# Gathering the rows of two experts at once, with the normed rows as stationary operand

## The chip, the core and the metric

The kernel runs on one core of one Trainium2 chip. The metric is the device time in microseconds of one execution, as a median of several runs. Everything is float32. TensorE (PE) multiplies, VectorE (DVE) and ScalarE (ACT) read the results from PSUM and write them to SBUF, GpSimd (POOL) has small jobs, and SyncE (SP) issues the transfers of the weights. In the tables of the profile a float32 matrix product stands as two MATMUL instructions, each with its own weight load (PEld), and a transpose on PE as one.

## What is computed

One layer of an encoder on 256 tokens of width 1024: two attention branches and their merge, then a mixture of 32 experts of which each token takes 4, then a last norm. The part that matters here is the mixture:

```python
h2 = rmsnorm(x, norm2_g[l])
logits = (xt @ w_router + b_router).astype(jnp.float32)
top_v, top_i = lax.top_k(logits, TOP_K)        # 4 of 32
gates = jax.nn.softmax(top_v, axis=-1)
...
def expert_block(args):                          # rows of the tokens of one expert
    xblk, e = args
    gu = xblk @ w_gu[e] + b_gu[e]                # 1024 -> 2048
    gate = jnp.minimum(gu[:, :D_EXPERT], SWIGLU_LIMIT)
    up = jnp.clip(gu[:, D_EXPERT:], -SWIGLU_LIMIT, SWIGLU_LIMIT)
    act = (up + 1.0) * (gate * jax.nn.sigmoid(SWIGLU_ALPHA * gate))
    return act @ w_down[e] + b_down[e]           # 1024 -> 1024
...
out = jnp.zeros((T + 1, D), jnp.float32).at[row_tok].add(row_w[:, None] * yb.astype(jnp.float32))
```

The weights of one expert are 12 MB: 8 MB for the first product, 4 MB for the second. The 32 experts read 403 MB.

## The kernel before

Each engine runs a program of its own, written out by hand, and semaphores order them. The weights come through a ring of 24 slots of 1 MB in SBUF (`ring`). An expert takes 12 of them: 8 for `up_tile` (one slot is one slice of 128 input channels, gate and up side by side) and 4 for `down_tile`. So the ring holds two experts. SP loads four slots at a time (a group, 4 MB, `group_load`), and a group may be loaded as soon as PE has counted its four slots as read on the semaphore `freed`; the first 24 slots are loaded singly while the attention runs, and the last four singly again. Slot 23 waits for the semaphore `opened`.

The mixture works on blocks of `CAP` = 64 rows for each expert. DVE makes `pick`, a one-hot matrix of tokens by slots, with `build_picks`. In the program `experts(i)` on PE one expert e has, in this order:

- 8 `up_tile`, each with four products (two halves of a bank of PSUM, for `UP` and `GATE`) on the turned rows `xT_e`, and among them the transpose of the routing weights (`turn_gated`) and the biases;
- `scatter`: four products that add the result of expert e-1 to the four banks with the sums of all tokens;
- `gather`: four products with `pick` (128 tokens by 64 slots) as stationary and 512 columns of the normed rows `h2` as moving operand, which put the rows of expert e+1 into the bank `Y`; ACT copies them to `x_e`;
- `turn(act_v)`: four transposes of the activations of e, which DVE then copies to `actT`;
- `turn(x_e, UP)`: four transposes of the rows of e+1, which ACT copies to `xT_e`;
- 8 `down_tile`, two for a slot, which free their slots; ACT copies the result to `y_e`.

The activations of e come from DVE and ACT (`clamp_up`, `clamp_gate`, sigmoid, two products on DVE) while PE scatters and gathers. Ahead of expert 0 stands a prologue: `gather(0, first=True)`, the last of four products that open the sums (`open_sums(1, 1)`, which raises `opened`), `turn(x_e)` and the transpose of all routing weights (`turn_gated(1, Y)`). PE, ACT and DVE loop over the experts two at a time (`UNROLL`), PE with the first and the last two written out.

## Time and profile before

| | before |
|---|---|
| median of 3 runs | 1141.51 us (1140.75 to 1142.64) |
| the profiled execution, its own time | 1142.35 us |
| its span from the first to the last instruction | 1140.4 us |
| mean granted clock of TensorE | 0.998 of full speed |
| PE busy | 1108.2 us, 97% of the span |
| DVE, ACT, POOL busy | 221.8 us, 146.2 us, 30.3 us |
| read from HBM | 433.14 MB, 381 GB/s over the span |

The experts begin at 231.65 us of the span and take nine tenths of what is left of it. PE is busy nearly all of the time, and so are the transfers; which of the two sets the end can't be read from such shares, only from who waits for whom. 1.95 us of the profiled execution's time lie outside its span.

### The profile page before, as it was taken

Reading aid. Unit: us, or ns where it says so; the run is one execution under the profiler, and the core shown is the slowest. Engines: PE = TensorE matmul, PEld = TensorE weight load, DVE = VectorE, ACT = ScalarE, POOL = GpSimd, SP = SyncE. Lnnn points to the kernel's source line nnn. Section 1 sums busy time; section 2 is a strip of 40 time slices with the busy share of each in tenths; the row PEclk is TensorE's granted clock in tenths of the full one; section 3 lists DMA queues with packets and bytes.
Section 4 is the critical chain, followed back from the end, with each engine's and each line's share of the span. In section 5 each row is a group of like instructions: output and inputs, shape, how many; then the busy total and the mean of one; then the engine's idle time right before and its main releaser. Section 6 shows DMA issues by size and latency. Waiting matters only on the chain.

```text
span 1140.4 us, 12368 instructions
## 1 busy us (share of the span) xinstructions
PE 1108.2 (97%) x5162; PEld 451.6 (40%) x5163; DVE 221.8 (19%) x548; ACT 146.2 (13%) x306; POOL 30.3 (3%) x43
## 2 busy tenths in 40 slices
PE   7999999999999999999999999999999999999997
PEld 5858887433333333333333333333333333333332
DVE  1264213321111111111111111111111111111112
ACT  1053120210001100000000000100000000000001
POOL 1250000000000000000000000000000000000000
PEclk9999999999999999999999999999999999999999
DMA  9944366489999999999999999999999999999993
GB/s 361 412 142 179 113 252 223 153 353 409 429 434 428 437 425 438 425 438 426 438 426 438 426 437 428 436 429 434 430 433 431 432 432 431 433 429 434 430 423 132
DMA packets 26725, 434.49 MB, mean 381 GB/s; under 512 B 6416, under 2 KB 6672, under 8 KB 8912
## 3 DMA queue, kind: packets, MB, share of 16 engines
q1 hardware_dynamic: 22208, 430.32, 89.2%
q10 hardware_dynamic: 4496, 3.87, 1.1%
q8 instruction: 15, 0.25, 0.1%
q14 instruction: 6, 0.05, 0.0%
HBM read 433.14 MB, written 1.05 MB: 381 GB/s over the span
## 4 chain that ended last, share of the span: by engine, by line
PE 75%; DMA 22%; ACT 2%; DVE 1%; issue 0%; POOL 0%; DVEq 0%; SPq 0%; POOLq 0%
PE ps L1313 30%; DMA ring<-in_up 21%; PE ps L1327 14%; PE ps L1152 5%; PE ps L1284 4%; PE ps L1335 4%; PE ps L1166 2%; PE ps L1229 2%; PE ps L1041 2%; PE ps L1322 2%; PE ps L1291 1%; ACT work L615 1%; PE ps L1096 1%; PE ps L1060 1%; PE ps L1031 1%; PE ps L1297 1%
## 5 line engine op out<-in xcount | busy, mean ns | idle before, releaser
L1313 PE MATMUL ps<-ring,work 128*64 128x512 f32 x2048 | 461.3, 596 | 12.1 <-DMA ring<-in_up 11.5
L1313 PEld LDWEIGHTS ps<-ring,work 128*64 128x64 f32 x2048 | 141.0, 137 | 301.4 <-issue 281.1
L1327 PE MATMUL ps<-ring,work 128*64 128x512 f32 x1024 | 226.8, 595 | 0.6
L905 DVE TENSOR_SCALAR work<-ps 128x512 f32<-128x512 f32 x32 | 22.1, 692 | 673.6 <-PE ps L1313 673.6
L1327 PEld LDWEIGHTS ps<-ring,work 128*64 128x64 f32 x1024 | 70.7, 137 | 136.1 <-issue 127.9
L1335 PE MATMUL ps<-work 64*128 64x512 f32 x264 | 65.6, 615 | 0.8 <-ACT work L643 0.8
L1284 PE MATMUL ps<-work 128*64 128x512 f32 x264 | 63.9, 605 | 0.1
L1152 PE MATMUL ps<-work,ring 128*128 128x256 f32 x256 | 56.6, 379 | 0.0
L618 ACT ACTIVATE work<-ps 128x256 f32<-128x256 f32 x33 | 12.6, 383 | 336.5 <-PE ps L1297 336.5
L615 ACT ACTIVATE work<-ps 128x512 f32<-128x512 f32 x66 | 39.4, 597 | 104.8 <-PE ps L1284 80.1
L1152 PEld LDWEIGHTS ps<-work,ring 128*128 128x128 f32 x256 | 48.5, 190 | 6.6
L1291 PE MATMUL ps<-const,work 128*128 128x128 f32 x260 | 42.7, 287 | 3.5
L643 ACT ACTIVATE work<-ps 128x512 f32<-128x512 f32 x32 | 19.1, 597 | 208.6 <-PE ps L1327 208.6
L1291 PEld LDWEIGHTS ps<-const,work 128*128 128x128 f32 x260 | 27.4, 141 | 37.6 <-issue 26.0
L637 ACT ACTIVATE work<-work 128x512 f32<-128x512 f32 x32 | 20.2, 630 | 163.4 <-DVE work L902 163.4
L1335 PEld LDWEIGHTS ps<-work 64*128 64x128 f32 x264 | 22.8, 186 | 43.1 <-issue 43.1
L956 DVE COPY work<-ps 128x512 f32<-128x512 f32 x32 | 22.1, 692 | 70.8 <-PE ps L1291 70.8
L1322 PE MATMUL ps<-work 32*64 32x512 f32 x256 | 34.8, 613 | 0.0
L1284 PEld LDWEIGHTS ps<-work 128*64 128x64 f32 x264 | 16.0, 136 | 44.1 <-issue 42.6
L1229 PE MATMUL ps<-ring 128*128 128x512 f32 x64 | 28.5, 595 | 0.0
L1166 PE MATMUL ps<-ring 128*128 128x256 f32 x128 | 28.1, 380 | 0.0
L484 POOL TENSOR_TENSOR sums<-sums,eps 128x1 f32<-128x1 f32 x4 | 2.2, 553 | 966.5 <-DVE sums L834 966.5
(156 smaller groups left out, 540.2 us busy)
## 6 DMA issues: line engine op xcount, KB each, us to landing
ring<-in_up SPq DMA_DIRECT2D x60, 4096.0 KB, 38.1
ring<-in_down SPq DMA_DIRECT2D x29, 4096.0 KB, 35.4
ring<-in_front SPq DMA_DIRECT2D x22, 1024.0 KB, 17.7
ring<-in_up SPq DMA_DIRECT2D x16, 1024.0 KB, 5.4
ring<-in_down SPq DMA_DIRECT2D x12, 1024.0 KB, 9.6
ring<-in_front SPq DMA_DIRECT2D x2, 832.0 KB, 7.9
ring<-in_x SPq DMA_DIRECT2D x2, 512.0 KB, 4.0
ring<-in_x ACTq DMA_DIRECT2D x1, 1024.0 KB, 4.8
```

The costliest lines, as they stand in the source:

```text
L615: return act.activation(dst, ps[:, bank, :], ACT.Copy)
L905: return dve.tensor_scalar(up_c, ps[:, UP, :], LIMIT, -LIMIT, ALU.min, ALU.max)
L1041: last = pe.matmul(ps[:, c // 2, c % 2 * SEQ:(c % 2 + 1) * SEQ], w[:, k % 2, c * P:(c + 1) * P], hT[:, k, :], start=k == 0 and c % 2 == 0, ...
L1152: last = pe.matmul(ps[:, 6 + g % 2, c * SEQ:(c + 1) * SEQ], w[:, k, c * P:(c + 1) * P], hT[:, k, :], start=k == 0, stop=k == KT - 1)
L1166: last = pe.matmul(ps[:, d % 4, m * SEQ:(m + 1) * SEQ], w[:, c, d % 4 * P:(d % 4 + 1) * P], oT[:, 4 * m + c, :], start=c == 0, stop=c == 3)
L1229: return pe.matmul(ps[:, 4 + 2 * t + n, :], gateT[:, k, t * P:(t + 1) * P], w[:, k % 2, n * BANK:(n + 1) * BANK], start=k == 0, stop=k == ...
L1284: last = pe.matmul(ps[n * CAP:(n + 1) * CAP, bank, :], pick[:, b, t, :], h2[:, t, n * BANK:(n + 1) * BANK], start=t == 0, stop=t == TT - 1)
L1291: last = pe.transpose(ps[:, bank, c * P:(c + 1) * P], rows[:, c * P:(c + 1) * P], ident)
L1313: last = pe.matmul(ps[n * CAP:(n + 1) * CAP, bank, :], lhs(xT_e, k), w[bank - GATE][:, n * BANK:(n + 1) * BANK], start=k == 0, stop=k == K ...
L1322: pe.matmul(ps[n * CAP:(n + 1) * CAP, bank, :], expert_row[rows, b, :], up_bias[rows, :], start=False, stop=False, skip_group_check=True)
L1327: last = pe.matmul(ps[n * CAP:(n + 1) * CAP, Y, :], lhs(actT, k), w[:, n * BANK:(n + 1) * BANK], start=k == 0, stop=k == KT - 1, skip_grou ...
L1335: return pe.matmul(ps[:, n, :], gatedT[rows, b, t, :], y_e[rows, :], start=False, stop=False, skip_group_check=True)
```

## The change

The stationary and the moving operand of the gather change places, and two experts are gathered together. A product now has 128 tokens by 128 channels of `h2` as stationary operand and `pick` for two experts (128 tokens by 2 x 64 slots) as moving operand, so the rows arrive in PSUM already turned. Each expert of a pair does half of the pair's eight channel slices for the next pair: one slice ahead of `turn(act_v)` and three behind it. `x_e`, its copy and its transposes are gone; ACT copies one bank for each expert to `xT`, where four half pairs have a place (`homes`). The bank is now `UP`, so that PE waits for DVE's `clamp_up` ahead of it. The last two experts gather nothing. In the prologue all eight slices of the first pair are gathered at once, and the transpose of all routing weights moves behind the second `up_tile` of expert 0. DVE builds the picks of a pair at once, and in the prologue it also copies half of the first pair's rows. The loops of PE, ACT and DVE now take four experts a turn (`UNROLL` is 4, `PAIR` is 2).

```diff
-UNROLL = RING // PER_EXPERT
+PAIR = RING // PER_EXPERT
-TURNS = E // UNROLL
+TURNS = E // PAIR
+UNROLL = 2 * PAIR
...
+        def homes(pair, high):
+
+            if pair % 2:
+                return xT[:, 2:4] if high else xT[:, 0:2]
+            return xT[:, 1:4:2] if high else xT[:, 0:3:2]
...
-            act.wait_ge(gathered, 1)
-            take(x_e).then_inc(xe_ready, 1)
-            act.wait_ge(xT_done, 1)
-            take(xT_e).then_inc(xT_ready, 1)
+            def take_xT(pair, high, bank=UP):
+                return act.activation(homes(pair, high).rearrange("p u k s -> p k u s"),
+                                      ps[:, bank, :].rearrange("p (k u s) -> p k u s", k=4, u=2), ACT.Copy)
+
+
+            act.wait_ge(gathered_low, 1)
+            take_xT(0, 0, MIX).then_inc(xT_ready, 1)
...
-                    act.wait_ge(gathered, e + 2)
-                    take(x_e, Y).then_inc(xe_ready, 1)
-                    act.wait_ge(xT_done, e + 2)
-                    take(xT_e, UP).then_inc(xT_ready, 1)
+                    if not (isinstance(i, int) and e >= E - PAIR):
+                        act.wait_ge(gathered, e + 2)
+                        take_xT(u // PAIR + 1, u % PAIR).then_inc(xT_ready, 1)
...
-            build_picks(0, 0).then_inc(pick_ready, 1)
+            build_picks(0, 0)
+            build_picks(1, 1).then_inc(pick_ready, 1)
             normed(1, 1)
-            build_picks(1, 1).then_inc(pick_ready, 1)
...
+            dve.wait_ge(gathered, 1)
+            dve.tensor_copy(homes(0, 1).rearrange("p u k s -> p k u s"), ps[:, Y, :].rearrange("p (k u s) -> p k u s", k=4, u=2)).then_inc(xT_high, 1)
...
+                    if u % PAIR == 0:
+
+                        dve.wait_ge(gathered, e + 1)
+                        build_picks(0, e + PAIR)
+                        build_picks(1, e + PAIR + 1).then_inc(pick_ready, 1)
...
-                    build_picks(u % 2, e + 2).then_inc(pick_ready, 1)
...
-            def gather(b, bank=MIX, first=False):
+            def picked(bank, q, k, t, first, last):
+
+                return pe.matmul(ps[:, bank, q * 2 * CAP:(q + 1) * 2 * CAP], h2[:, t, k * P:(k + 1) * P], pick[:, t, :], start=first, stop=last,
+                                 skip_group_check=True)
+
+            def gather_first():
+
                 for t in range(TT):
-                    if first:
-                        pe.wait_ge(h2_ready, 2 * t + 2)
-                    for n in range(2):
-                        last = pe.matmul(ps[n * CAP:(n + 1) * CAP, bank, :], pick[:, b, t, :], h2[:, t, n * BANK:(n + 1) * BANK],
-                                         start=t == 0, stop=t == TT - 1)
+                    for k in range(KT):
+                        if k % 4 == 0:
+                            pe.wait_ge(h2_ready, 2 * t + k // 4 + 1)
+                        last = picked((MIX, Y)[k // 4], k % 4, k, t, t == 0 and k % 4 == 0, t == TT - 1)
+                        if t == TT - 1 and k == 3:
+                            last.then_inc(gathered_low, 1)
+                last.then_inc(gathered, 1)
+
+            def gather(k):
+
+                for t in range(TT):
+                    last = picked(UP, k % 4, k, t, t == 0, t == TT - 1)
+                return last
...
-            gather(0, first=True).then_inc(gathered, 1)
+            gather_first()
             open_sums(1, 1).then_inc(opened, 1)
-            pe.wait_ge(xe_ready, 1)
-            turn(x_e).then_inc(xT_done, 1)
-
-            pe.wait_ge(first_gates, 1)
-            turn_gated(1, Y).then_inc(first_ps, 1)
...
-                        up_tile(b, k, use(k), up_done).then_inc(freed, 1)
+                        if static and e == 0 and k == 4:
+                            pe.wait_ge(xT_high, 1)
+                        up_tile(homes(pair, k // 4)[:, b, k % 4, :], k, use(k), up_done).then_inc(freed, 1)
+                        if static and e == 0 and k == 1:
+
+                            pe.wait_ge(first_gates, 1)
+                            turn_gated(1).then_inc(first_ps, 1)
...
+                    following = not (static and e >= E - PAIR)
                     pe.wait_ge(y_ready, e + 1)
                     for n in range(2 * TT):
                         scatter(1 - b, n)
-                    pe.wait_ge(pick_ready, e + 2)
-                    gather(1 - b, Y).then_inc(gathered, 1)
+                    if following:
+                        if b == 0:
+                            pe.wait_ge(pick_ready, i * (UNROLL // PAIR) + (pair + 2))
+                        pe.wait_ge(clamped2, e + 1)
+                        gather(4 * b)
                     pe.wait_ge(gT_ready, e + 1)
                     pe.wait_ge(act_ready, e + 1)
                     turn(act_v).then_inc(actT_done, 1)
-                    pe.wait_ge(xe_ready, e + 2)
-                    turn(x_e, UP).then_inc(xT_done, 1)
+                    if following:
+                        for k in range(4 * b + 1, 4 * b + 4):
+                            last = gather(k)
+                        last.then_inc(gathered, 1)
                     pe.wait_ge(actT_ready, e + 1)
...
-            with pe.Fori(1, TURNS - 1) as i:
+            with pe.Fori(1, E // UNROLL - 1) as i:
                 experts(i)
-            experts(TURNS - 1)
+            experts(E // UNROLL - 1)
```

What this makes of PE's order at two places. First the prologue and the start of expert 0, before (L1284 is `gather`, L1224 `open_sums`, L1291 `turn`, L1297 `turn_gated`, L1313 `up_tile`; here a product is one row):

```order
81 L1224 MATMUL ps<-ring,const 128x512
82 L1284 MATMUL ps<-work 64x512 x4
83 L1224 MATMUL ps<-ring,const 128x512
84 L1291 MATMUL ps<-const,work 128x128 x4
85 L1297 MATMUL ps<-const,work 128x128 x2
86 L1313 MATMUL ps<-ring,work 64x512 x24
87 L1297 MATMUL ps<-const,work 128x128 x2
```

and the same place now (L1299 is the new gather, L1243 `open_sums`, L1335 `turn_gated`, L1351 `up_tile`):

```order
81 L1243 MATMUL ps<-ring,const 128x512
82 L1299 MATMUL ps<-work 128x128 x16
83 L1243 MATMUL ps<-ring,const 128x512
84 L1351 MATMUL ps<-ring,work 64x512 x8
85 L1335 MATMUL ps<-const,work 128x128 x2
86 L1351 MATMUL ps<-ring,work 64x512 x16
87 L1335 MATMUL ps<-const,work 128x128 x2
```

Four wide products and four transposes have become 16 narrow products, and the two transposes of the routing weights now stand behind the second `up_tile`. Second the middle of an expert on PE, before (L1322 the biases, L1335 `scatter`, L1284 `gather`, L1291 both `turn`s, L1327 `down_tile`):

```order
89 L1322 MATMUL ps<-work 64x512 x4
90 L1313 MATMUL ps<-ring,work 64x512 x4
91 L1335 MATMUL ps<-work 128x512 x4
92 L1284 MATMUL ps<-work 64x512 x4
93 L1291 MATMUL ps<-const,work 128x128 x8
94 L1327 MATMUL ps<-ring,work 64x512 x16
```

and now (L1373 `scatter`, L1299 the gather, L1329 `turn(act_v)`, L1365 `down_tile`):

```order
89 L1360 MATMUL ps<-work 64x512 x4
90 L1351 MATMUL ps<-ring,work 64x512 x4
91 L1373 MATMUL ps<-work 128x512 x4
92 L1299 MATMUL ps<-work 128x128 x2
93 L1329 MATMUL ps<-const,work 128x128 x4
94 L1299 MATMUL ps<-work 128x128 x6
95 L1365 MATMUL ps<-ring,work 64x512 x16
```

The four products of 512 columns and the second four transposes are gone, and eight products of 128 columns stand around the first four transposes.

## Rows read from the trace of the kernel before

**Rows 1.** The page, part 4: the chain that ended last, by engine

```profile
PE 75%; DMA 22%; ACT 2%; DVE 1%; issue 0%; POOL 0%; DVEq 0%; SPq 0%; POOLq 0%
```

**Rows 2.** Stretches: length, busy PE, PEld, DVE, ACT, POOL; clock, DMA share, GB/s

```profile
260.00:320.00 60.00, 59.75 (x284) 19.67 (x282) 8.80 (x20) 5.78 (x11) 0.00 (x0) 1.00 1.00 425
...
980.00:1100.00 120.00, 114.47 (x540) 36.99 (x538) 17.60 (x40) 11.22 (x20) 0.00 (x0) 1.00 1.00 432
```

**Rows 3.** Chain that ended last, 960 to 1110 us: start, length, what

```profile
1002.38 49.16 DMA ring<-in_up
...
1060.40 49.43 DMA ring<-in_up
```

**Rows 4.** PE's waits after 255 us: total, times, longest

```profile
PE ps L1313 <- DMA ring<-in_up: 11.5, 10, 1.3
```

**Rows 5.** DMA from 300 to 400 us: instruction queue; transfers, KB, us to landing

```profile
q8 instruction: 2, 0.03, 0.1%
...
ring<-in_up SPq DMA_DIRECT2D x7, 4096.0 KB, 22.0
```

**Rows 6.** The same from 400 to 1050 us, where only one queue is listed

```profile
q1 hardware_dynamic: 9636, 280.66, 100.3%
...
ring<-in_up SPq DMA_DIRECT2D x46, 4096.0 KB, 41.7
```

**Rows 7.** Timeline of SP's issues: start, length, what

```profile
238.92 8.90 SPq L381 DMA_DIRECT2D ring<-in_up  x2
259.72 0.33 SPq L381 DMA_DIRECT2D ring<-in_down  x1
...
287.39 0.33 SPq L381 DMA_DIRECT2D ring<-in_down  x1
```

**Rows 8.** Half microseconds: the stretch, clock, DMA share, GB/s at its end

```profile
260.00:260.50 0.50, 0.50 (x4) 0.14 (x2) 0.00 (x0) 0.17 (x1) 0.00 (x0) 1.00 0.01 0
```

**Rows 9.** Timeline of the prologue and expert 0, PE and DVE

```profile
226.85 0.42 DVE L891 TENSOR_SCALAR work<-const,places 128x64 f32<-128x64 f32 x2
...
227.33 1.94 PE L1284 MATMUL ps<-work 128*64 128x512 f32 x8
...
231.65 10.52 PE L1313 MATMUL ps<-ring,work 128*64 128x512 f32 x48 [0.60 <-ACT work L615]
...
247.22 1.99 PE L1335 MATMUL ps<-work 64*128 64x512 f32 x8
...
252.44 7.09 PE L1327 MATMUL ps<-ring,work 128*64 128x512 f32 x32
```

**Rows 10.** Timeline of PE and PEld at 128x128 stationary operands

```profile
208.06 1.04 PE L1205 MATMUL ps<-const,ring 128*128 128x128 f32 x8
208.93 1.88 PE L1229 MATMUL ps<-ring 128*128 128x512 f32 x4
...
214.65 0.19 PEld L1229 LDWEIGHTS ps<-ring 128*128 128x128 f32 x1 [0.24 <-issue]
...
224.10 0.39 PE L1269 MATMUL ps<-work 128*128 128x32 f32 x2
...
224.32 0.39 PE L1270 MATMUL ps<-work 128*128 128x32 f32 x2
```

**Rows 11.** Timeline of the last expert on DVE: the activations

```profile
1120.15 0.69 DVE L954 TENSOR_TENSOR work<-work 128x512 f32<-128x512 f32 x1
```

**Rows 12.** Chain that ended last, in the last expert

```profile
1113.53 0.37 PE ps L1297 x2
...
1118.65 1.92 PE ps L1335 x8
1120.57 1.89 PE ps L1284 x8
...
1122.48 0.61 ACT work L615
...
1123.13 0.66 PE ps L1291 x4
```

More of the change, by code:

```diff
@@ L162, in build @@
         soft = sb("soft", [P, 2, 8])
-        routing = sb("routing", [P, TT, E + UNROLL])
+        routing = sb("routing", [P, TT, E + PAIR])
         places = sb("places", [P, TT, ROUNDS * E])
@@ L217, in build @@
         h2 = held(0, TT, D)
-        x_e = held(2048, BANK)
-        xT_e = held(2560, BANK)
-        gate_c, up_c, sig, y_e = (held(3072 + n * BANK, BANK) for n in range(4))
+        xT = held(3072, 4, 4, CAP)
+        xT_over = held(3072, KT, CAP)
+        gate_c, up_c = (held(2048 + n * BANK, BANK) for n in range(2))
+        sig, y_e = (held(4096 + n * BANK, BANK) for n in range(2))
         actT, act_v = gate_c, up_c
-        pick = held(5120, 2, TT, CAP)
+        pick = held(5120, TT, 2 * CAP)
         gated = held(5376, 2, TT, P)
@@ L233, in build @@
         part_rows = held(3744, TT, P)
[L234 to L236 removed]
+        logits, struck = (held(4096 + n * TT * (E + TOP), TT, E + TOP) for n in range(2))
+        best, strike = (held(4240 + n * TT * 8, TT, 8) for n in range(2))
+        chosen, expo = (held(4272 + n * TT * E, TT, E) for n in range(2))
         gf = flat[:, PER_EXPERT * SLOT:PER_EXPERT * SLOT + D]
@@ L317, in through, with fine @@
             return FIRST[name] + dict(FRONT)[name]
+        def homes(pair, high):
+            if pair % 2:
+                return xT[:, 2:4] if high else xT[:, 0:2]
+            return xT[:, 1:4:2] if high else xT[:, 0:3:2]
+        def fine(turn, at):
+            return turn == 0 or turn == TURNS - 1 and at >= RING - SPAN
         block = ctx.enter_context(nc.Block())
@@ L381, in group_load, with fine_load @@
                 sp.dma_start(ring[:, SPAN * g:SPAN * (g + 1), :], unit(i, g)).then_inc(grouped[g], 16)
+            def fine_load(i, at):
+                sp.wait_ge(freed, i * RING + (N_FRONT - RING + at + 1))
+                expert_load(i, at)
             with sp.Fori(1, TURNS - 1) as i:
@@ L659, in _ @@
                             act.wait_ge(v_gathered, k + 1)
-                            take(x_e).then_inc(v_xe, 1)
-                            act.wait_ge(v_xTd, k + 1)
-                            take(xT_e).then_inc(v_xT, 1)
+                            act.activation(xT_over, ps[:, MIX, :].rearrange("p (k s) -> p k s", k=KT), ACT.Copy).then_inc(v_xT, 1)
                             act.wait_ge(v_gTd, k + 1)
@@ L890, in build_picks @@
                 for t in range(TT):
-                    last = dve.tensor_scalar(pick[:, b, t, :], slots, places[:, t, bass.ds(je, 1)], None, ALU.is_equal)
+                    last = dve.tensor_scalar(pick[:, t, b * CAP:(b + 1) * CAP], slots, places[:, t, bass.ds(je, 1)], None, ALU.is_equal)
                 return last
@@ L1355, in experts @@
                     b = u % 2
+                    pair = u // PAIR
                     def use(j):
-                        at = u * PER_EXPERT + j
-                        if isinstance(i, int) and (i == 0 or at >= RING - SPAN):
-                            pe.wait_ge(loaded[at], 16 * (front_loads(at) + 1 + (i > 0)))
+                        at = u % PAIR * PER_EXPERT + j
+                        turn = i * (UNROLL // PAIR) + pair
+                        if static and fine(turn, at):
+                            pe.wait_ge(loaded[at], 16 * (front_loads(at) + sum(fine(n, at) for n in range(turn + 1))))
                         elif at % SPAN == 0:
-                            pe.wait_ge(grouped[at // SPAN], i * 16)
+                            pe.wait_ge(grouped[at // SPAN], i * (16 * UNROLL // PAIR) + 16 * (pair))
                         return halves(at)
                     for k in range(KT):
-                        up_tile(b, k, use(k), up_done).then_inc(freed, 1)
+                        if static and e == 0 and k == 4:
[4 more added lines that the diff above has]
+                            turn_gated(1).then_inc(first_ps, 1)
                         if k == 5:
                             pe.wait_ge(gated_ready, e + 1)
+                            if static and e == 0:
+                                pe.wait_ge(y_ready, 1)
                             turn_gated(b).then_inc(gT_done, 1)
@@ L1409, in _ @@
                             pe.wait_ge(v_pick, k + 1)
-                            gather(0).then_inc(v_gathered, 1)
-                            pe.wait_ge(v_xe, k + 1)
-                            turn(x_e).then_inc(v_xTd, 1)
+                            gather_over().then_inc(v_gathered, 1)
                             pe.wait_ge(v_xT, k + 1)
@@ L1416, in _ @@
                             for j in range(KT):
-                                last = up_tile(0, j, halves(j), v_up)
+                                last = up_tile(xT_over[:, j, :], j, halves(j), v_up)
                                 if j == 0:
```

38 lines of the change are left out of this document (19 added, 19 removed).

## Prediction

> **What bounds the kernel now.** I read the chain that ended last first. It gives PE three quarters of the span and the transfers 22% [rows 1], and a busy PE beside a busy DMA says no more. So I went along the chain in order of time. In its last third it has a piece of transfer of some 49 us in each turn of two experts, which ends at 1051.54 and again at 1109.83 us [rows 3]: 58.29 us for two experts, 29.15 us for one. SP's issues show the other rate: a down group is issued when PE has freed its slots, at 259.72 and at 287.39 us [rows 7], so early on PE needs 27.67 us for an expert. PE is the faster one, by 1.48 us an expert. It doesn't wait at first because the ring starts full, and it eats this lead up.
>
> Three more views say that the transfers are the limit all along. The DMA share is 1.00 from 260 us on, with 425 to 432 GB/s, whether PE waits or not [rows 2]. The time from issue to landing of an up group grows from 22.0 us (300 to 400 us) to 41.7 us (400 to 1050 us) [rows 5, 6], where 4 MB alone take 4.19 MB / 432 GB/s = 9.7 us: orders pile up in the queue. And PE's waits for the weights come to 11.5 us in all [rows 4]; that is the whole sum by which PE would be ahead. The time then is: when the transfers become continuous, plus a fixed 90 groups less two, plus what PE does after the last up group has landed.
>
> The Trainium skill, page "DMA: Bandwidth & Descriptors", section "Where 436 GB/s comes from", puts the ceiling of the ports at 435 GB/s. By that the 432 GB/s can't get better, and no faster PE draws more from them.
>
> **The price of a narrow product.** The new instruction is a load of 128x128 float32 and 128 moving columns; a product is two of them. Before has none exactly so. Eight transposes, each with a load of 128x128 and 128 moving columns, take 208.93 - 208.06 = 0.87 us until the next product starts, 0.109 us each [rows 10]. Products with the same stationary operand and only 32 columns, two instructions, follow each other at 0.22 us (224.10, 224.32), 0.11 each [rows 10]. The load of 0.19 us hides behind 0.43 us of 512 columns (0.19 busy, 0.24 idle) [rows 10]. I take 0.112 us. From below it can't be under 0.107, since 512 columns take 0.43. From above, load and pass one after the other would be 0.19 + 0.107 = 0.297 us; loads that follow each other but hide the pass, 0.19. The short pairs lie at the low end.
>
> **An expert on PE.** Before, from the start of `scatter` to the start of `down_tile`: 252.44 - 247.22 = 5.22 us [rows 9]. In it lie gather 1.89, the wait for ACT's copy 0.61 and the turn of `x_e` 0.66 [rows 12]. Now: scatter 1.92, first slice 4 x 0.112 = 0.45, turn of the activations 4 x 0.109 = 0.43, three slices 12 x 0.112 = 1.34; in all 4.14 us, a gain of 1.08 an expert. Do new waits appear? The activations are ready at 1120.15 + 0.69 = 1120.84, 2.2 us after the scatter's start at 1118.65 [rows 11, 12]; PE is there after 2.37. DVE's copy to `actT` (a pass over 512 columns like that of 0.69 us [rows 11]) hides behind the three slices (1.34); without them it would be the wait it is in the tail below. `clamp_up` is over before the scatter ends. ACT's copy has the 7.09 us of `down_tile`, and DVE's four picks stand where DVE waits for PE. So 27.67 becomes 26.59 us, against 29.15 for the transfers. These 31 x 1.08 = 33.5 us go into PE's wait for weights, which becomes 11.5 + 33.5 = 45 us, and not into the time.
>
> **The prologue.** DVE makes two picks (0.42 us) before PE starts at 227.33, and the second pair of picks comes ahead of it now [rows 9]: PE starts at 227.75. 32 instructions x 0.112 = 3.58, `open_sums` two passes at 0.43 = 0.86: expert 0 starts at 232.19 instead of 231.65 [rows 9]. ACT's copy of the low half (behind 24 instructions, at 230.44, plus 0.6) is done by then; DVE's half, at 231.3 plus 0.7, is wanted 7 us later. The routing sums that DVE now does behind this copy are wanted behind the second `up_tile`, 3.6 us after the start. The transposes of the routing weights add 0.37 [rows 12] ahead of the third slot. The first group is freed 0.54 + 0.37 = 0.91 us later, and SP issues it at 239.8 instead of 238.92 [rows 7]. `opened` comes 2 us later too; slot 23 is wanted only at the end of expert 1, and behind it the DMA had been idle before 238.92 anyway.
>
> The second group is queued behind the first, so both end 0.91 later. The third, issued at 259.72 [rows 7], changes by 0.91 - 1.08 = -0.2. Before, nothing moved from 260.0 to 260.5 [rows 8], between the end of the second and the start of the third; with the third already queued this gap of about 0.6 us goes. The transfers become continuous 0.91 - 0.6 = 0.3 us later (between -0.6, if the start of the pipe shortens too, and 0.9).
>
> **The tail.** The last up group lands at 1109.83 [rows 3]. The last expert gathers nothing: from 1120.57 PE would go to the turn of the activations at about 1120.9, and then takes 0.66 + 0.69 + 0.08 = 1.43 for turn, copy and start. `down_tile` starts at 1122.3 instead of 1123.79 (1123.13 + 0.66 [rows 12]): 1.5 us less. Its weights, 9.7 us behind the last up group, are there at 1119.5.
>
> **Sum.** + 0.3 - 1.5 = - 1.2 us. On the profiled execution: span 1140.4 to 1139.2, with the 1.95 us outside it 1142.35 to 1141.2. The median of the runs stands 0.8 us below that execution: 1141.5 - 1.2 = 1140.3 us. A difference of 0.2% (2.3 us) is about what can be told from no change; this is under it.
>
> **The rivals.**
>
> *PE is the bound, and gets its gain.* The chain's 75% speak for it: -33.5 - 1.2 gives 1106.8 us. Against it stand the landing times and the DMA share. 3 in 100.
>
> *The transfers gain too.* At 260 to 320 us they had 425 GB/s and later 432 [rows 2]. If a queue that fills sooner cures that, it is 60 x 7 / 432 = 1.0 us; with the gap gone and no delay at the front (-0.6), the sum is -0.6 - 1.0 - 1.5 = -3.1: 1138.4 us. For it speaks only that the slow stretch is the one with few orders waiting. 12 in 100.
>
> *Slower: the stationary load isn't hidden.* At price x an expert costs 16 (x - 0.112) more. PE has 45 us to give away over 31 experts, 496 instructions: up to x = 0.112 + 45/496 = 0.203 only the prologue's 32 instructions count (at 0.19 us +2.5, which gives 1142.8, no measurable change). Beyond it PE is the bound. At 0.297: 496 x 0.185 - 45 = +46.8, prologue +5.9, rest -1.2, so 1193 us. It decides at 0.203. Against it is 0.109 of the transposes. 6 in 100.
>
> The Trainium skill speaks for this rival: page "TensorE: Matmul & The Clock Gate", section "The mechanism", says that a weight load overlaps running products only when its row group differs (or, a sentence earlier, in the background buffer). Here all use all rows, so by the stricter sentence it would be 0.297 and 1193 us. The 0.43 spacing with 0.19 of load in it contradicts that sentence.
>
> *Slower: the transfers lose rate.* PE now reads four times as many stationary columns for the gather while the weights stream in. If they stayed at the 425 GB/s of the first stretch [rows 2] for the 850 us of the stream, it is 850 x 7 / 432 = +14 us, 1154 us. In these rows the rate doesn't follow what PE does. 3 in 100.
>
> *Slower: the longer loop is fetched again at each turn.* Before, 400 to 1050 us list no instruction queue at all [rows 6], while 300 to 400 still has two packets [rows 5]; the body stays, with 130 MATMULs and as many loads an expert and two experts, some 520 instructions. Now it is 134 and 134 for each of four, about 1070. With five jumps back and 45 us to give away, a jump must cost over 9 us to be seen; at 10 us each the time is 1140.3 + 5 = 1145. 2 in 100.
>
> The Trainium skill, page "Runtime: NRT & Kernel Launch", section "Instruction fetch mechanics", says that a jump out of a window of two pages of 256 instructions stalls. The body before is already beyond two pages, and no fetch is seen.
>
> **How the numbers follow.** My case has 74 in 100; its own range is 1139.2 (both bounds low, -0.6 - 1.5 and x = 0.107) to 1142.8 (x = 0.19). The faster cases, with 1138.4, are taken in below; above, the scatter of the runs themselves, 1140.75 to 1142.64, is added to 0.6 of delay. Range 1138.2 to 1143.4. Faster by over 0.2% means under 1139.2: 3 + 12 = 15. Slower, over 1143.8: 6 + 3 + 2 = 11. Within: 74.
>
> **What would show it.** Right: an expert's PE work from scatter to `down_tile` at 4.1 us; 32 instructions of the prologue in 3.6 us; PE's waits for weights near 45 us and beginning before 600 us; the last up group landing within 1 us of 1109.8 at 432 GB/s; from there to the end 29.1 instead of 30.6 us. Wrong: a spacing near 0.3 us in the gather, an expert's period over 29.15 us with no DMA wait, instruction packets between 400 and 1050 us with idle PE, or a DMA share under 1.00 after 260 us.

## The result and the profile after

The changed kernel is a little slower: 1143.59 us against 1141.64 us (medians of 17 runs each), a ratio of 1.0018 with a 95% interval of 1.0010 to 1.0025, that is +2.0 us (1.1 to 2.9). Forecast was -1.2 us, with a range of 1138.2 to 1143.4 us. The profiled execution after took 1143.02 us, its span is 1141.2 us; for the one of before that is 1142.35 and 1140.4 us.

The chain that ended last, by engine, and the stretches of the profile after (columns as in [rows 2]):

```profile
PE 59%; DMA 38%; DVE 1%; ACT 1%; issue 0%; POOL 0%; DVEq 0%; SPq 0%; POOLq 0%
```

```profile
260.00:320.00 60.00, 60.00 (x302) 22.16 (x300) 8.88 (x20) 5.01 (x9) 0.00 (x0) 1.00 1.00 428
...
500.00:620.00 120.00, 120.00 (x598) 44.31 (x596) 17.76 (x40) 9.81 (x18) 0.00 (x0) 1.00 1.00 433
620.00:740.00 120.00, 114.49 (x562) 41.35 (x560) 19.01 (x42) 8.83 (x16) 0.00 (x0) 0.99 1.00 431
...
980.00:1100.00 120.00, 110.61 (x528) 38.96 (x525) 17.77 (x40) 8.23 (x15) 0.00 (x0) 0.97 1.00 431
```

The transfers run as before, at 431 to 433 GB/s [rows 2]. New is the clock: from 620 us on its mean is under 1.00. PE's waits, the transfers' landing between 400 and 1050 us, and SP's issues (a queue of the kind "instruction" carries code to an engine; I call its entries code packets, and the profile doesn't say for which engine they are):

```profile
PE ps L1351 <- DMA ring<-in_up: 25.0, 17, 2.8
```

```profile
q8 instruction: 3, 0.05, 0.0%
q14 instruction: 1, 0.01, 0.0%
...
ring<-in_up SPq DMA_DIRECT2D x47, 4096.0 KB, 48.7
```

```profile
240.45 8.89 SPq L393 DMA_DIRECT2D ring<-in_up  x2
260.35 0.33 SPq L393 DMA_DIRECT2D ring<-in_down  x1
...
287.13 0.33 SPq L393 DMA_DIRECT2D ring<-in_down  x1
```

The orders pile up higher (48.7 instead of 41.7 us, [rows 6]), an expert takes PE 26.78 us (260.35 to 287.13) instead of 27.67 [rows 7], and PE waits 25.0 us instead of 11.5 [rows 4], the first time at 643 us and not before 600. PE's timeline of the prologue, of expert 0 and of its end:

```profile
228.02 3.84 PE L1299 MATMUL ps<-work 128*128 128x128 f32 x32 [0.46 <-DVE work L903]
231.69 1.02 PE L1243 MATMUL ps<-ring,const 128*128 128x512 f32 x2
232.65 3.65 PE L1351 MATMUL ps<-ring,work 128*64 128x512 f32 x16
236.23 0.44 PE L1335 MATMUL ps<-const,work 128*128 128x128 f32 x2
...
248.74 1.99 PE L1373 MATMUL ps<-work 64*128 64x512 f32 x8
250.66 0.71 PE L1299 MATMUL ps<-work 128*128 128x128 f32 x4
251.20 0.60 PE L1329 MATMUL ps<-const,work 128*128 128x128 f32 x4
251.64 1.50 PE L1299 MATMUL ps<-work 128*128 128x128 f32 x12
253.07 7.09 PE L1365 MATMUL ps<-ring,work 128*64 128x512 f32 x32
```

From `scatter` to `down_tile` it is 253.07 - 248.74 = 4.33 us (5.22 before), and the loads of 128x128 are hidden: 32 instructions in 3.67 us, 0.115 each.

**Where an execution differs by chance.** Two profiles of one kernel differ already in the attention part, and this moves everything behind it. The first products start at 6.94 to 7.24 us, by when x has landed; more comes from the 32 instructions behind the first transposes, which take 12.42 us in the first profile of the changed kernel and 11.39 us in its second. Why isn't shown. So the stages are counted from a mark: the start of the first products of the output projection (L1229, now L1248). The table takes them from the profile of each run; "first group" is SP's first group of four slots, "last up" the landing of the last up group, "down" the start of the last eight down tiles. "Last wait" is PE's wait ahead of the last up group. The kernels below the fourth row are those of the experiments.

| kernel | mark | first group - mark | last up - mark | last wait | last up to down | down to end |
|---|---|---|---|---|---|---|
| before | 190.89 | 48.03 | 918.94 | 1.26 | 13.97 | 16.6 |
| before, again | 191.07 | 48.03 | 918.95 | 1.24 | 13.97 | 16.6 |
| after | 191.26 | 49.19 | 919.55 | 1.03 | 12.66 | 17.7 |
| after, again | 190.25 | 49.19 | 919.72 | 2.75 | 14.36 | 17.8 |
| fill_end | 190.08 | 49.19 | 919.77 | 0.21 | 12.67 | 16.6 |
| pad_real | 190.90 | 49.19 | 919.54 | 2.64 | 12.67 | 16.6 |
| before_tail | 189.93 | 48.02 | 919.06 | 1.25 | 12.57 | 16.5 |
| fine_turn1 | 190.03 | | 916.62 | 3.06 | 14.08 | 17.5 |
| best | 190.31 | | 916.52 | 0.22 | 12.66 | 16.5 |
| prologue_twice | 190.20 | 52.76 | 923.10 | 2.65 | 14.36 | 16.5 |
| pad_pe | 191.11 | 49.19 | 919.50 | 0.99 | 12.67 | 17.7 |
| pad_act | 189.82 | 49.19 | 919.50 | 2.65 | 14.31 | 18.0 |
| fill_end2 | 189.82 | 49.19 | 919.52 | 0.20 | 12.67 | 16.6 |
| pad_early | 190.65 | 49.19 | 921.91 | 0.99 | 12.67 | 16.6 |

Three columns tell of the change: the last group lands 0.6 to 0.8 us later, the way to the last down tiles is 1.3 us shorter or 0.4 us longer, and what follows is 1.1 to 1.2 us longer.

### The profile page after: what moved, and what is told of

Read it like the earlier page. It is cut to its first block, busy times and chain, and to the rows that moved or that the text cites. A ratio compares the mean times of both kernels' runs of the same rounds, so it can differ in the third digit from the quotient of the medians.

```text
span 1141.2 us, 12513 instructions
## 1 busy us (share of the span) xinstructions
PE 1095.8 (96%) x5278; PEld 482.9 (42%) x5279; DVE 223.8 (20%) x549; ACT 125.4 (11%) x271; POOL 30.3 (3%) x43
## 4 chain that ended last, share of the span: by engine, by line
PE 59%; DMA 38%; DVE 1%; ACT 1%; issue 0%; POOL 0%; DVEq 0%; SPq 0%; POOLq 0%
DMA ring<-in_up 38%; PE ps L1351 24%; PE ps L1365 9%; PE ps L1171 5%; PE ps L1299 3%; PE ps L1185 2%; PE ps L1248 2%; PE ps L1060 2%; PE ps L1373 2%; PE ps L1360 2%; PE ps L1115 1%; PE ps L1079 1%; PE ps L1050 1%; PE ps L1335 1%; PE ps L1088 1%; PE ps L1329 1%
## 5 line engine op out<-in xcount | busy, mean ns | idle before, releaser
L1351 PE MATMUL ps<-ring,work 128*64 128x512 f32 x2048 | 474.8, 609 | 25.0 <-DMA ring<-in_up 25.0
L1351 PEld LDWEIGHTS ps<-ring,work 128*64 128x64 f32 x2048 | 142.2, 139 | 326.1 <-issue 285.9
L1365 PE MATMUL ps<-ring,work 128*64 128x512 f32 x1024 | 226.8, 595 | 1.6 <-DVE work L976 1.6
L1365 PEld LDWEIGHTS ps<-ring,work 128*64 128x64 f32 x1024 | 70.6, 137 | 133.7 <-issue 128.0
L1299 PEld LDWEIGHTS ps<-work 128*128 128x128 f32 x512 | 61.8, 191 | 24.0 <-issue 22.7
L1299 PE MATMUL ps<-work 128*128 128x128 f32 x512 | 70.3, 281 | 0.5 <-DVE work L903 0.5
L1373 PE MATMUL ps<-work 64*128 64x512 f32 x264 | 65.6, 615 | 0.7 <-ACT work L657 0.7
L1171 PE MATMUL ps<-work,ring 128*128 128x256 f32 x256 | 56.6, 379 | 0.0
L1171 PEld LDWEIGHTS ps<-work,ring 128*128 128x128 f32 x256 | 48.5, 190 | 6.6
L657 ACT ACTIVATE work<-ps 128x512 f32<-128x512 f32 x32 | 19.1, 597 | 212.0 <-PE ps L1365 212.0
L1373 PEld LDWEIGHTS ps<-work 64*128 64x128 f32 x264 | 22.7, 186 | 43.1 <-issue 41.5
L634 ACT ACTIVATE work<-ps 128x512 f32<-128x512 f32 x31 | 18.5, 597 | 93.6 <-PE ps L1299 93.6
L1248 PE MATMUL ps<-ring 128*128 128x512 f32 x64 | 28.5, 595 | 0.0
L1060 PE MATMUL ps<-work,ring 128*128 128x256 f32 x128 | 27.8, 379 | 0.0
L1060 PEld LDWEIGHTS ps<-work,ring 128*128 128x128 f32 x128 | 24.3, 190 | 3.6 <-issue 0.3
```

The source lines that it names most:

```text
L1060: last = pe.matmul(ps[:, c // 2, c % 2 * SEQ:(c % 2 + 1) * SEQ], w[:, k % 2, c * P:(c + 1) * P], hT[:, k, :], start=k == 0 and c % 2 == 0, ...
L1171: last = pe.matmul(ps[:, 6 + g % 2, c * SEQ:(c + 1) * SEQ], w[:, k, c * P:(c + 1) * P], hT[:, k, :], start=k == 0, stop=k == KT - 1)
L1248: return pe.matmul(ps[:, 4 + 2 * t + n, :], gateT[:, k, t * P:(t + 1) * P], w[:, k % 2, n * BANK:(n + 1) * BANK], start=k == 0, stop=k == ...
L1299: return pe.matmul(ps[:, bank, q * 2 * CAP:(q + 1) * 2 * CAP], h2[:, t, k * P:(k + 1) * P], pick[:, t, :], start=first, stop=last, skip_gr ...
L1351: last = pe.matmul(ps[n * CAP:(n + 1) * CAP, bank, :], x, w[bank - GATE][:, n * BANK:(n + 1) * BANK], start=k == 0, stop=k == KT - 1, skip ...
L1365: last = pe.matmul(ps[n * CAP:(n + 1) * CAP, Y, :], lhs(actT, k), w[:, n * BANK:(n + 1) * BANK], start=k == 0, stop=k == KT - 1, skip_grou ...
```

## The experiments

**The two kernels again.**

> The kernel before, once more, to see which differences of two single profiles are the draw of one execution. Three such differences lie between the profile of before and that of after: the attention part starts 0.36 us later in after, already at the first matrix product behind the load of x; the output stores have a hole of 1 us; the last up group lands 0.97 us later. Every theory: ratio 1.000 within 0.1%. If the first two are draws, they differ between the two profiles of before as well, by 0.3 us and about 1 us.

Measured: 1141.75 us, ratio 0.9999 (0.9990 to 1.0008). Its stages are those of before to 0.02 us; only the mark moved. So the slow end of the stores, which I had thought a draw of one execution, is none.

> The changed kernel, once more. Theory A (clock): PE now waits longer for each up group, and behind such waits its granted clock falls to half for some 3 us, as at 1081.67 us of the first profile, where 16 up products took 5.32 instead of 3.65 us. In the stream that costs nothing, but behind the very last wait it lengthens the tail by 1.67 us. Then this profile should show the fall behind the last up group in some executions, and the ratio is 1.0018 again. Theory B (prologue): the delay at the first group, 1.2 us net of the draw, is all there is; then the span from the last up group to the end is 29.2 us plus the draw of the stores, and the ratio can't be over 1.000.

Measured: 1144.08 us, ratio 1.0021 (1.0012 to 1.0030). Theory A's fall of the clock is there behind the last up group. PE's up tiles behind a wait, in the two profiles of the changed kernel (first the first one, with the turns before; then the second):

```profile
818.04 5.35 PE L1351 MATMUL ps<-ring,work 128*64 128x512 f32 x16 [2.15 <-DMA ring<-in_up]
847.18 3.65 PE L1351 MATMUL ps<-ring,work 128*64 128x512 f32 x16 [0.44 <-DMA ring<-in_up]
876.33 5.35 PE L1351 MATMUL ps<-ring,work 128*64 128x512 f32 x16 [2.16 <-DMA ring<-in_up]
...
1052.54 3.65 PE L1351 MATMUL ps<-ring,work 128*64 128x512 f32 x16 [2.79 <-DMA ring<-in_up]
1081.67 5.32 PE L1351 MATMUL ps<-ring,work 128*64 128x512 f32 x16 [2.13 <-DMA ring<-in_up]
1110.85 3.65 PE L1351 MATMUL ps<-ring,work 128*64 128x512 f32 x16 [1.03 <-DMA ring<-in_up]
```

```profile
1080.75 3.65 PE L1351 MATMUL ps<-ring,work 128*64 128x512 f32 x16 [2.15 <-DMA ring<-in_up]
1110.01 5.35 PE L1351 MATMUL ps<-ring,work 128*64 128x512 f32 x16 [2.75 <-DMA ring<-in_up]
```

and the stretches of 1 us of the second (clock third from the end):

```profile
1109.00:1110.00 1.00, 0.00 (x0) 0.00 (x0) 0.00 (x0) 0.00 (x0) 0.00 (x0) 1.00 0.95 393
1110.00:1111.00 1.00, 0.99 (x4) 0.44 (x6) 0.00 (x0) 0.00 (x0) 0.00 (x0) 0.66 0.96 401
1111.00:1112.00 1.00, 1.00 (x4) 0.24 (x2) 0.00 (x0) 0.00 (x0) 0.00 (x0) 0.50 1.04 434
1112.00:1113.00 1.00, 1.00 (x4) 0.24 (x2) 0.00 (x0) 0.00 (x0) 0.00 (x0) 0.50 1.02 426
```

The 16 instructions take 3.65 us, or 5.35 us with the clock at 0.50 (1.2 GHz instead of 2.4), and never the longer time behind a wait of 0.44 us. Behind a wait of over 2 us the clock mostly falls, not always: behind 14 of the 19 such waits of these two profiles. In the stream it costs nothing: the 1.7 us come out of the next wait, which is then 0.4 us. Behind the last wait they are paid. In the first profile the clock fell one wait earlier, at 1081.67 us, so that the last wait was only 1.03 us long and no fall followed; in the second it fell behind the last wait itself. The same holds for the other profiles in which no wait was filled: behind a last wait of 2.65 to 3.06 us it fell (fine_turn1, pad_act, prologue_twice), behind one of 0.99 us it didn't (pad_pe, pad_early). Only pad_real, with a last wait of 2.64 us and no fall, stands out.

**The gather in the experts twice.**

```diff
             def gather(k):

-                for t in range(TT):
-                    last = picked(UP, k % 4, k, t, t == 0, t == TT - 1)
+                for _ in range(2):
+                    for t in range(TT):
+                        last = picked(UP, k % 4, k, t, t == 0, t == TT - 1)
```

> The changed kernel with each narrow product of the gather inside the experts issued twice (the second overwrites the first with the same numbers; the prologue gathers once): 16 x 0.112 = 1.8 us more PE work for an expert, 28.6 us against 29.15 for its transfers, so PE's waits nearly vanish. Theory A (clock behind waits): faster than the changed kernel by 1 to 2 us, ratio to before 0.999 to 1.000, and a mean clock of 0.998. Theory B (prologue): the same as the changed kernel, ratio 1.0018, since the prologue and the tail are unchanged. If PE were the bound it would be 30 x 1.8 = 54 us slower.

Measured: 1153.85 us, ratio 1.0109 (1.0094 to 1.0125), and no wait of PE for weights at all.

```profile
307.36 1.16 PE L1299 MATMUL ps<-work 128*128 128x128 f32 x8
308.36 0.60 PE L1330 MATMUL ps<-const,work 128*128 128x128 f32 x4
308.79 2.84 PE L1299 MATMUL ps<-work 128*128 128x128 f32 x24
311.57 7.09 PE L1366 MATMUL ps<-ring,work 128*64 128x512 f32 x32
```

Both expectations were wrong, because I compared one expert with one transfer and forgot the lead that the full ring gives the transfers at the start. 16 instructions more cost 1.79 us an expert (28.57 instead of 26.78), for 30 experts 53.7 us. The median is 9.8 to 10.3 us over the changed kernel's, but this run has neither of the two extra costs at the end that are found below (16.6 us from down to end, mean clock 0.999). By the stages, the last down tiles start 944.5 us after the mark instead of 932.2 (after) and 932.4 (fill_end), 12.1 to 12.3 us later. So PE had 41.4 to 41.6 us to give away, where the prediction has 45. What the clock costs it can't tell.

**Single loads in the second turn.**

```diff
         def fine(turn, at):

-            return turn == 0 or turn == TURNS - 1 and at >= RING - SPAN
+            return turn <= 1 or turn == TURNS - 1 and at >= RING - SPAN
...
-            with sp.Fori(1, TURNS - 1) as i:
+            for at in range(RING):
+                fine_load(1, at)
+            with sp.Fori(2, TURNS - 1) as i:
...
-                            pe.wait_ge(grouped[at // SPAN], i * (16 * UNROLL // PAIR) + 16 * (pair))
+                            pe.wait_ge(grouped[at // SPAN], i * (16 * UNROLL // PAIR) + 16 * (pair) - 16)
```

> The changed kernel with the 24 slots of the second turn loaded singly, each as soon as PE has freed it, instead of four at a time. Both theories have the transfers as the bound from 260 us on: they now go on as soon as slot 0 is free (234.5 us) and slot 23 has landed (about 237 us), instead of at 240.45 us, so the last up group lands 3 to 4 us earlier, if the single loads keep 432 GB/s, and the time falls by as much: ratio to before 0.998 to 0.999. If the gap of the DMA between 236.8 and 240.5 us were hidden anyway, nothing changes.

Measured: 1140.74 us, ratio 0.9996 (0.9987 to 1.0005), 3.3 us under the changed kernel beside it. The last up group lands 3.0 us earlier after the mark. The stretches behind 236 us of this kernel, and of the changed one:

```profile
236.00:238.00 2.00, 2.00 (x13) 0.58 (x8) 0.84 (x6) 0.00 (x0) 0.00 (x0) 1.00 0.97 373
238.00:240.00 2.00, 2.00 (x12) 0.72 (x10) 0.00 (x0) 0.00 (x0) 0.00 (x0) 1.00 0.98 315
```

```profile
236.00:238.00 2.00, 2.00 (x12) 0.75 (x12) 1.29 (x7) 0.38 (x1) 0.00 (x0) 1.00 0.34 143
238.00:240.00 2.00, 2.00 (x12) 0.66 (x10) 0.06 (x1) 0.00 (x0) 0.00 (x0) 1.00 0.00 0
```

The changed kernel's transfers stand still from 237 to 241 us, here they don't: of these 4 us some 3 come back at the end.

**The waits at the end filled.**

```diff
+                        if static and e >= E - UNROLL and k == 3:
+                            for n in range(10 if e == E - 1 else 8):
+                                pe.matmul(ps[:, MIX, 0:P], h2[:, n % TT, 0:P], ident, start=True, stop=True)
```

> The changed kernel with idle work on PE in the last four experts, between the fourth and the fifth up tile, where it waits for the second up group: 8 narrow products of h2 and the identity into the bank MIX (10 in the last expert), 1.8 and 2.2 us, whose result nobody reads. Theory A (the clock falls behind the last wait): PE's wait ahead of the last up group falls from 2.75 us to some 0.5 us, the clock stays up behind it, the 16 products take 3.65 instead of 5.35 us, and the median falls by 1.2 to 1.7 us: ratio 1.0005 to 1.001. Rival (the clock is harmless in the timed executions): no change, 1.002. If the filling is too long it adds at most its excess over the wait, under 1 us.

Measured: 1140.96 us, ratio 0.9993 (0.9984 to 1.0002). That is 0.0025 to 0.0028 under the changed kernel's ratios (1.0018, 1.0021), 2.9 to 3.2 us and not 1.7.

```profile
1107.18 2.50 PE L1412 MATMUL ps<-const,work 128*128 128x128 f32 x20
1109.89 3.65 PE L1351 MATMUL ps<-ring,work 128*64 128x512 f32 x16 [0.21 <-DMA ring<-in_up]
```

The clock stayed up; but the stores were fast again too, which this edit wasn't meant to do. The issue and landing of the four stores (duration of an issue in ns, min/median/max; landing in us), first of the changed kernel, then of this one:

```profile
L696 ACTq DMA_DIRECT2D out<-ring x4: 362/414/967, 1135.4 to 1137.9; - x4
...
DMA to landing us min/median/max: 2.6/3.0/3.3
```

```profile
L696 ACTq DMA_DIRECT2D out<-ring x4: 338/350/374, 1134.4 to 1136.6; - x4
...
DMA to landing us min/median/max: 2.1/2.1/2.1
```

In the changed kernel a code packet comes among the stores, between 1136 and 1137 us; in fill_end there is none after 1132 us:

```profile
q8 instruction: 1, 0.02, 7.0%
```

**Idle instructions.** 128 `pe.nop()` ahead of PE's first wait; and 64 `act.nop()` ahead of ACT's first use of the latents.

> The changed kernel with 128 idle instructions at the head of PE's program, where PE waits 7 us for x. It shifts the places at which PE's program is fetched in pieces. In both profiles of the changed kernel a code packet comes 1 to 2 us ahead of the third output store, one store takes 0.97 or 1.61 us to issue instead of 0.35, the stores land after 3.0 instead of 2.1 us and the DMA stands still for about 1 us; in both of before, and in the kernel with the gather issued twice, none of this is there. Theory C (a fetch of PE's code at the end of its program meets the stores): the packet moves away, the stores are issued in 0.35 us each, and the end comes 1.2 us sooner after the start of the last down tiles (16.6 instead of 17.7 us). Rival (the fetch is another engine's, or the stores are slow for another reason): 17.7 us again.

> The changed kernel with 64 idle instructions in ACT's program, where it waits 16 us for the first products. The same for ACT's program: if the fetch ahead of the stores is ACT's, which also issues the stores, it moves away and the end comes 16.6 instead of 17.7 us after the start of the last down tiles. If it is PE's, 17.7 us again.

Measured: pad_pe 1143.49 us, ratio 1.0018 (1.0009 to 1.0028); pad_act 1143.43 us in its one run. 17.7 and 18.0 us from down to end, code packets as in the changed kernel. The count of executed instructions is 12513 in both, as in the changed kernel, so no idle instruction was executed: these two are the changed kernel once more and test neither theory. As such pad_pe is of use: it ran beside fill_end on one chip and is 2.5 us slower.

**The shorter tail alone, in the kernel before.** Its last expert leaves out `gather`, `turn(x_e, UP)` and ACT's two copies.

> The kernel before with one part of the change alone: its last expert gathers nothing, turns and copies no rows for a next one. From the last up group to the start of the last down tiles it should take 12.7 us (as in the changed kernel without a fall of the clock) instead of 13.97, and the transfers and the prologue stay, so 1.3 us faster, ratio 0.9989, if no code fetch meets the stores. If the tail isn't on the path, 1.000.

Measured: 1139.86 us, ratio 0.9983 (0.9974 to 0.9992). 12.57 instead of 13.97 us in the profile, the rest unchanged to 0.1 us. This part of the change is worth 1.4 us by the stages and 1.9 us (0.9 to 3.0) by the medians.

**PE's program longer by real instructions.** In pad_real 32 idle products in expert 28 alone, written like those of fill_end.

> The changed kernel with 32 idle narrow products (128 instructions of PE's program, 3.6 us) in expert 28 alone, ahead of its second up group, where PE waits some 3 us anyway; PE has 2.4 us an expert to catch up before expert 31. The idle instructions of the runs before this one left the count of executed instructions at 12513, so they moved no code; these do, by nearly as much as the filling of the last four experts (136). Theory C (code fetch at the end of PE's program meets the stores): the stores land after 2.1 us, and from the start of the last down tiles to the end it takes 16.6 us, while the clock behind the last wait may still fall; ratio 1.0005 to 1.001. Rival (the stores were slow because the clock had fallen or PE had waited): 17.7 us, 1.002.

Measured: 1142.67 us, ratio 1.0008 (0.9999 to 1.0017).

```profile
1110.49 3.65 PE L1351 MATMUL ps<-ring,work 128*64 128x512 f32 x16 [2.64 <-DMA ring<-in_up]
```

```profile
DMA to landing us min/median/max: 2.1/2.1/2.1
```

The stores are fast, though PE waited 2.64 us and the last waits were not filled: so it is the length of PE's program that counts for them. Nor do slow stores come with the fall of the clock: in pad_pe and the first profile of the changed kernel they are slow without it, in prologue_twice (below) they are fast with it. The profiled execution of pad_real, without a fall, was with 1141.5 us the fastest of ten; the others reach 1143.3.

In fill_shift the filling of the last four experts and 30 products more in expert 28:

> The filling of the last four experts, with 30 more products in expert 28, so that PE's program is 256 instructions longer than the changed kernel's instead of 136. Theory C, with the place of the code counting modulo 256 instructions: the code packet is back ahead of the stores, which land after 3.0 us, and 17.7 us pass from the last down tiles to the end; the clock stays up, as with the filling: 1142.1 us, 1.2 us more than with the shorter filling. If the slow stores came with the fall of the clock: 16.6 us, 1141.0 us.

Measured: 1146.94 us, ratio 1.0053 (1.0038 to 1.0068). The 76 instructions took 8.7 us, and PE was still late at the last up group, so the time compares with nothing. The stores landed after 2.6 to 3.6 us, with a code packet among them, and 18.1 us passed from down to end.

In prologue_twice each product of the first gather stands twice:

> The changed kernel with each product of the first gather issued twice (the copy goes to a bank that nobody reads): 32 instructions, 3.6 us more ahead of expert 0. Theory (the transfers are the bound, and a delay of the first group moves them all): the first group is issued 3.6 us later, counted from the first products of the output projection 52.8 instead of 49.2, and the last up group lands 3.6 us later, 923.3 instead of 919.6. Rival (the ring's lead hides the prologue): 919.6 again.

Measured: 1146.05 us in its one run. First group 52.76 and last up 923.10 us after the mark: 3.57 us later there, 3.4 to 3.6 us later here. A delay of the prologue goes to the end one to one. The clock fell behind the last wait (14.36), and the stores landed after 2.1 us.

The version best has the edits of fine_turn1 and fill_end together:

> Single loads in the second turn and the filling of the last four experts together. The single loads brought the last up group 3.3 us forward, the filling took 3.1 us off the changed kernel (clock 1.7, stores 1.2). If both add up: 1144.0 - 6.4 = 1137.6 us, ratio 0.996 to 0.997 to the kernel before.

Measured: 1138.01 us, ratio 0.9968 (0.9956 to 0.9981): 3.6 us faster than the kernel before. Both edits add up (the 3.3 us of the expectation are the difference of the medians; the last up group itself had come 3.0 us forward), and this version beats both kernels.

**Clock and code apart.** pad_early has 17 idle products in each of the experts 2 and 3 and none at the end; fill_shift2 has 15 in each of these and the filling at the end.

> The filling of the last four experts once more, as the partner of the two others on the same chip: 1141.0 us as before, ratio 0.9993, stores landing after 2.1 us, no fall of the clock behind the last wait.

> The changed kernel with the same 34 idle products in experts 2 and 3 instead of the last four: PE's program is as long as that of the filling, PE has given the 3.8 us back long before the end, and the waits at the end are those of the changed kernel. Theory: stores land after 2.1 us as with the filling, since only the place of the code counts; the clock may fall behind the last wait, as in four of seven profiles with such waits, so the median lies between that of the filling and 1.7 us above it, near 1.0: 1142.0 us, ratio 1.000 to 1.001. If the clock played no part in the timed executions, it would be the filling's median.

> The filling of the last four experts and 30 idle products in experts 2 and 3: PE's program is 256 instructions longer than the changed kernel's, and the waits at the end are filled. Theory (the place of the code in pieces of 256): the code packet comes between the stores again, they land after some 3.0 us, and 17.7 us pass from the last down tiles to the end; the median is 1.2 us above that of the filling. Rival (any longer program cures it): 16.6 us and the filling's median.

Measured: fill_end2 1141.67 us, ratio 0.9998 (0.9989 to 1.0007); pad_early 1143.56 us, 1.0014 (1.0005 to 1.0023); fill_shift2 1143.53 us, 1.0012 (1.0003 to 1.0021). Both others lost time ahead of the end, which the comparison was to leave equal: the 16 instructions on the last up group start 921.95 and 921.18 us after the mark, 2.4 and 1.6 us later than in fill_end2 (919.56). In pad_early the weights came late: the idle products of 4 us held back SP's groups in experts 2 and 3 while few orders were queued, and from 350 to 352 us the DMA share was 0.77. In fill_shift2 PE didn't wait for these weights at all and was late itself: its last wait was at 994.25 us, with the clock down behind it. So the medians don't tell the clock and the code apart. The profile does tell of the stores: in fill_shift2 17.8 us from down to end, landing as below, with the packet back between 1136 and 1137 us; in pad_early 16.6 us.

```profile
L696 ACTq DMA_DIRECT2D out<-ring x4: 362/410/1012, 1136.1 to 1138.7; - x4
...
DMA to landing us min/median/max: 2.6/3.1/3.3
```

With 0 and 256 instructions more in PE's program the stores are slow, with 64 (prologue_twice), 128, 136 and 320 (gather_twice) they are fast. That the length of PE's program decides, and that a code packet stands among the slow stores each time, is shown. That the packet is PE's own fetch is the likely reading, and how it would slow another engine's stores isn't shown.

## Why the prediction was wrong

**What bounds the kernel: right.** The transfers ran on at their rate, PE's gain went into its waits, and all that counts is the start of the stream and what follows its end (prologue_twice, fine_turn1, before_tail).

**The narrow product: right.** 0.115 us instead of 0.112, and an expert 26.78 instead of 26.59 us, so the gain was 0.89 us an expert and not 1.08. The stricter sentence on weight loads that the prediction quotes from the Trainium skill, page "TensorE: Matmul & The Clock Gate", section "The mechanism", doesn't hold here: all these products use all row groups, and their loads are hidden.

**The prologue: right in kind, 0.3 to 0.5 us too small.** Expected was +0.91 us at the first group, measured +1.16: expert 0 starts 0.63 us later after the mark (0.54 expected; the 32 instructions took 3.67 us instead of 3.58), and from there to the group's issue it takes 0.53 us more (0.37 expected). The hole behind the second group did close, for +1.16 became +0.6 to +0.8 at the last up group. The sum had +0.3.

**The tail: right.** -1.5 expected, -1.3 measured without the fall of the clock.

**"These 31 x 1.08 = 33.5 us go into PE's wait for weights, ... and not into the time": this step failed.** The waits were to become 45 us and measured 25.0. With 0.89 us an expert the gain is 27.6 us and not 33.5, which makes 39 us; and seven groups of 16 instructions at half clock took 1.7 us more each, together 12 us. 25.0 and 12 are 37 us, near the 39 and the 41.5 of gather_twice. So the waits aren't free: behind most of the long ones PE's clock falls to half for some 3 us. In the stream that only shortens the next wait, but the last wait has no later one to pay from: 1.7 us where the clock falls. It fell there in four of the eight profiles in which the last waits weren't filled (the changed kernel's second, fine_turn1, pad_act, prologue_twice; not its first, pad_pe, pad_real, pad_early), which makes 0.85 us as a mean. The medians say more, with more noise. Filling the waits brings the ratio to 0.9993 and 0.9998, against 1.0008 for pad_real with the same stores: 1.1 to 1.7 us, but from different chips and with intervals of 1 us to either side on each. On one chip, fill_end is 2.5 us under pad_pe; less 1.15 us for the stores that leaves 1.4 us. The Trainium skill, page "TensorE: Matmul & The Clock Gate", section "HAM oscillation — how this bites in real kernels", tells of such a fall behind waits for transfers, with longer waits than those of 2.1 to 2.8 us that were enough here; the sum should have asked what longer waits do to the tail.

**What stood in no term: the stores.** +1.1 to +1.2 us, because PE's program has another length, with which a code packet meets the output stores. The prediction weighed the fetches of the longer loop and rightly found them harmless: beside the four packets between 400 and 1050 us the transfers kept their 432 GB/s. It looked at no other place. The Trainium skill, page "Runtime: NRT & Kernel Launch", section "Instruction fetch mechanics", calls the crossing of a block "mostly hidden"; if the packet is such a crossing, at this place it wasn't.

Together: +0.7 - 1.3 + 1.15 + (0.85 to 1.7) = +1.4 to +2.3 us; measured +2.0 (1.1 to 2.9). Without the two that were missed it would have been -0.6 us; fill_end, which has neither, measured -0.8 us (-1.8 to +0.2) and, repeated on another chip, -0.2 us (-1.0 to +0.8). A gain of that size can hardly be told from no change, and these runs don't show it safely.

Open stays how often the clock falls behind the last wait. In seven of the eight profiles it went by the turn: where it had fallen behind the wait before, the last one was short and no fall came. What decides at which wait the alternation begins, and why pad_real stands out, isn't known.

## What to carry to other kernels

Where the transfers are the bound, look for gains only where their stream begins and behind its end; a faster engine in between gains nothing and buys longer waits. Ask of each such wait what the clock of PE does behind it, above all behind the last one, and fill it with idle products if need be. A change that only makes a program longer or shorter can move a code fetch into a critical place and cost a microsecond: where 0.1% matters, compare the stages of two profiles of each kernel before believing a median.

## What the runs showed of the hardware

- PE's clock fell to 0.50 behind waits of 2.1 us (16 instructions in 5.35 instead of 3.65 us), in a regular alternation with waits of 0.4 us, but not behind every wait of 2.1 to 2.8 us: behind 14 of 19 waits of over 2 us in the two profiles of the changed kernel, and behind none of the 1.26 us of the kernel before.
- Products with a stationary operand of 128x128 float32 and 128 moving columns follow each other at 0.115 us an instruction; their loads of 0.19 us are hidden.
- In the executions where a code packet came between the stores, the slowest issue of a store took 0.60 to 1.61 us instead of 0.38, and the stores landed after 2.7 to 3.2 us (medians) instead of 2.1.
- The attention part moved whole executions by up to 1.4 us (mark at 189.82 to 191.26 us): by up to 0.3 us at the first products, which wait for x, and by up to 1.1 us in 32 of the next MATMUL instructions (11.39 to 12.49 us, with a granted clock of 1.00 on record throughout).
